# Sample states, pooling and norm sums moved out of the mixer end and under the two input products

## Chip, cores and metric

The kernel runs on one core of a Trainium2 chip. The metric is the device time of one execution in microseconds.

## The reference

One decoder layer for 1024 prompt tokens and 8 sample tokens (1032 together), width 1024, all in float32. The part that the change touches is the mixer:

```python
h = rmsnorm(x, g_mix[l]); proj = h @ w_in[l]
qr, fr, ir, gr, u = jnp.split(proj, ...)           # five blocks of 512 columns
logf = jnp.log(lb + (1.0 - lb) * jax.nn.sigmoid(fr))
kk = (1.0 - lb) * jax.nn.sigmoid(-fr); qq = jax.nn.silu(qr)
o, S = hgrn2_chunked(qq, kk, ir, logf, s_hgrn[l])  # S = diag(f) S + outer(1 - f, i), o = S^T q
o = o * lax.rsqrt(jnp.mean(o * o, axis=-1, keepdims=True) + EPS) * hgrn_norm[l]
y_a = o * jax.nn.sigmoid(gr)
y_b = pool_mix(multiscale_pool(u, past)) * pool_scale[l]   # trailing means over 2, 4, 8, 16 rows
x = x + jnp.concatenate([y_a, y_b], axis=-1) @ w_out[l]
```

Each of the 8 sample tokens has its own old state of 4 heads, 128 x 128, and 15 past rows of u. Cross attention over 256 memory tokens and a SwiGLU block follow.

## The kernel before

The program is written by hand per engine; each engine runs its own list in order, and semaphores join them. TensorE is PE, VectorE is DVE, ScalarE is ACT, GpSimd is POOL, SyncE's queue is SP.

A product is made in stripes of 128 output channels. Each stripe has three thirds of 344 tokens (`chunk`), and each third is 24 matmuls: operands are split into a rounded part and a rest (`w_hi`, `w_lo`, `x_hi`, `x_lo`), and three of the four cross products are summed. For each stripe SP loads the weights into `raw` (two slots), POOL multiplies them by the norm's gains (`gain_stripe`), ACT rounds them into `w_hi` (`split_next`), DVE makes the rest `w_lo` (`split_lo`), and DVE empties each third from its bank (`plain_evac`). A new `raw` may be loaded when the rest of two stripes before is made. ACT rounds a stripe's weights one stripe ahead of its use.

The first stage `qfi` makes q, f and i in 12 stripes. The second, `gu`, makes g and u in 8 stripes, and under each of them lies one step of the recurrence over 128 tokens: TensorE turns the decayed keys and a copy `iv` of v that POOL makes (`turn`, L1664 and L1666), then makes scores and reads the state. For the step of the next stripe ACT makes `lf` and exponentials (`gates`), and DVE runs a scan (`decays`) and four products (`weigh`).

After `gu` comes the mixer end (`mixer_end` on each engine): the new sample states one token at a time, their reads, pooling on POOL (`pooling`, log-step sums in the buffers `pa` and `pb`) with the means on DVE (`means`, L1253), the sums of squares of o (L1746), the norm factors, gating, the pool mix (L1758), and the split of y into `y_hi` and `y_lo`. Only then does the output product start. What POOL's sum for group g may overwrite is guarded by `pooled`, the count of means that DVE has made:

```python
if g and l == (g - 1) % 2:
    pool.wait_ge(pooled, g)
```

Below, "stripe n" of `gu` counts from 0 to 7, and its start is the start of its first third.

## Time and profile before

| | |
|---|---|
| time, three runs | 1551.0 us median (1550.93 to 1552.17) |
| profiled execution | 1551.01 us, span 1549.3 us |
| busy: TensorE, VectorE, ScalarE, GpSimd | 97%, 49%, 21%, 23% of the span |
| mean granted clock of TensorE | 0.99 |
| mixer end | 302.05 to 351.75 us |

A row of the timeline gives start, duration, engine, line, operation, output and inputs with their shapes, a count, and in brackets the idle time before it with what ended it. A matmul on plain float32 shows as two records, a transpose or a matmul on rounded operands as one. Windows give the busy time of PE, PEld (weight loads), DVE, ACT and POOL, each with its count, then the granted clock of TensorE, the share of the DMA engines and GB/s.

### The profile page before, as it was taken

The page shows a single profiled execution, that of the slowest core. Times are in us where ns is not written, and L with a number is a line of the kernel's source. Part 1 is how long each engine was busy: PE and PEld are TensorE (multiplying, and loading weights), DVE is VectorE, ACT ScalarE, POOL GpSimd, SP SyncE. Part 2 cuts the span into 40 slices and gives each one's busy share as a digit, 9 for nine tenths or more (in the row PEclk, how much of TensorE's full clock was granted, in tenths as well). Part 3 has the DMA queues.
Part 4 walks back from the last instruction along what each step waited for, and adds up shares of the span by engine and source line. Part 5 has one row for each costly group of instructions (what it writes and reads, how often), then busy time and mean ns, then how long its engine had stood idle before and what let it go on. Part 6 is the DMA issues. An engine that isn't in the chain of part 4 may idle for free.

```text
span 1549.3 us, 24672 instructions
## 1 busy us (share of the span) xinstructions
PE 1504.4 (97%) x9751; PEld 1465.4 (95%) x9751; DVE 765.6 (49%) x1293; ACT 328.0 (21%) x482; POOL 361.3 (23%) x324
## 2 busy tenths in 40 slices
PE   7999999979999998999999999999999999999998
PEld 6999999949999987779999999999999999999998
DVE  5222666597754276548854454334445422344424
ACT  4023333371020133420121111001111100111111
POOL 2111211154542063005531110001111000111063
PEclk8999999999999998999999999999999999999999
DMA  5111100321151267131111111111111111112113
GB/s 164 42 54 41 42 27 27 81 82 42 41 149 55 68 192 230 64 114 42 54 42 52 43 51 44 41 54 41 45 49 44 51 42 55 41 41 68 34 48 110
DMA packets 155009, 100.98 MB, mean 65 GB/s; under 512 B 9508, under 2 KB 147748, under 8 KB 154947
## 3 DMA queue, kind: packets, MB, share of 16 engines
q1 hardware_dynamic: 154955, 100.24, 21.5%
q8 instruction: 36, 0.59, 0.2%
q14 instruction: 18, 0.15, 0.0%
HBM read 91.50 MB, written 8.96 MB: 65 GB/s over the span
## 4 chain that ended last, share of the span: by engine, by line
PE 84%; DVE 3%; ACT 1%; issue 1%; DMA 0%; DVEq 0%; POOL 0%; SPq 0%; ACTq 0%; POOLq 0%
PE pm L1610 25%; PE pm L1612 24%; PE pm L1611 24%; PE pm L1893 2%; PE pm L1820 2%; PE pm L1918 1%; DVE ssc L1409 1%; PE pm L1679 1%; PE pm L1691 1%; PE pm L1881 1%; PE pm L1717 0%; PE pm L1693 0%; PE pm L1676 0%; DVE vc L1405 0%; PE pm L1983 0%
## 5 line engine op out<-in xcount | busy, mean ns | idle before, releaser
L1610 PE MATMUL pm<-x_hi,w_hi 128*128 128x344 f32 x1728 | 556.1, 322 | 0.2 <-DVE proj L1144 0.2
L1612 PE MATMUL pm<-x_hi,w_lo 128*128 128x344 f32 x1728 | 552.1, 320 | 0.0
L1611 PE MATMUL pm<-x_lo,w_hi 128*128 128x344 f32 x1728 | 552.0, 319 | 0.0
L1610 PEld LDWEIGHTS pm<-x_hi,w_hi 128*128 128x128 f32 x1728 | 324.9, 188 | 1.7 <-issue 0.5
L1611 PEld LDWEIGHTS pm<-x_lo,w_hi 128*128 128x128 f32 x1728 | 324.8, 188 | 0.2
L1612 PEld LDWEIGHTS pm<-x_hi,w_lo 128*128 128x128 f32 x1728 | 325.0, 188 | 0.0
L792 ACT ACTIVATE w_hi<-raw 128x1024 fp32r<-128x1024 f32 x120 | 127.2, 1060 | 855.7 <-PE pm L1612 762.9
L644 POOL TENSOR_TENSOR raw<-raw,gains 128x1024 f32<-128x1024 f32 x72 | 137.9, 1917 | 717.6 <-DMA raw<-in_w_ffn_in 563.6
L1610 PE MATMUL pm<-s_hi,w_hi 128*128 128x344 f32 x528 | 168.9, 320 | 0.0
L1612 PE MATMUL pm<-s_hi,w_lo 128*128 128x344 f32 x528 | 168.7, 319 | 0.0
L1611 PE MATMUL pm<-s_lo,w_hi 128*128 128x344 f32 x528 | 168.5, 319 | 0.0
L1110 DVE TENSOR_TENSOR w_lo<-raw,w_hi 128x1024 fp32r<-128x1024 f32 x112 | 148.8, 1328 | 11.6 <-ACT w_hi L792 11.6
L1610 PEld LDWEIGHTS pm<-s_hi,w_hi 128*128 128x128 f32 x528 | 99.2, 188 | 0.0
L1612 PEld LDWEIGHTS pm<-s_hi,w_lo 128*128 128x128 f32 x528 | 99.2, 188 | 0.0
L1144 DVE TENSOR_TENSOR fa<-pm,rb 128x344 f32<-128x344 f32 x66 | 34.0, 516 | 132.0 <-PE pm L1612 128.6
L1611 PEld LDWEIGHTS pm<-s_lo,w_hi 128*128 128x128 f32 x528 | 99.1, 188 | 0.0
L1144 DVE TENSOR_TENSOR fp<-pm,rb 128x344 f32<-128x344 f32 x66 | 34.1, 516 | 114.6 <-PE pm L1612 114.6
L1144 DVE TENSOR_TENSOR proj<-pm,rb 128x344 f32 (+1 forms) x60 | 30.7, 514 | 114.0 <-PE pm L1612 114.0
L1573 DVE TENSOR_TENSOR acc<-pm,acc 128x344 f32 (+1 forms) x42 | 21.7, 517 | 101.1 <-PE pm L1612 101.1
L1610 PE MATMUL pm<-y_hi,w_hi 128*128 128x344 f32 x192 | 61.5, 320 | 0.7 <-issue 0.7
L1610 PE MATMUL pm<-o_hi,w_hi 128*128 128x344 f32 x192 | 61.6, 321 | 0.0
L1612 PE MATMUL pm<-y_hi,w_lo 128*128 128x344 f32 x192 | 61.3, 319 | 0.0
(261 smaller groups left out, 1969.0 us busy)
## 6 DMA issues: line engine op xcount, KB each, us to landing
raw<-in_w_ffn_in SPq DMA_DIRECT2D x44, 512.0 KB, 3.9
raw<-in_w_in SPq DMA_DIRECT2D x20, 512.0 KB, 3.8
vc<-in_cache_mem_v SPq DMA_DIRECT2D x16, 512.0 KB, 4.3
raw<-in_w_ffn_out SPq DMA_DIRECT2D x16, 512.0 KB, 3.9
xt<-in_x_prompt SPq DMA_DIRECT2D x8, 512.0 KB, 6.0
raw<-in_w_out SPq DMA_DIRECT2D x8, 512.0 KB, 3.9
raw<-in_w_cq SPq DMA_DIRECT2D x8, 512.0 KB, 3.9
vc<-in_cache_mem_k SPq DMA_DIRECT2D x8, 512.0 KB, 5.3
```

Of the source, the lines that this page charges most:

```text
L644: pool.tensor_tensor(raw[:, s, :, :], raw[:, s, :, :], g, ALU.mult).then_inc(gain_on, 1)
L792: act.activation(w_hi[s][:, :, :], src, ACT.Copy).then_inc(hi_made, 1)
L1110: dve.tensor_tensor(w_lo[s][:, :, :], raw[:, s, :, :], w_hi[s][:, :, :].bitcast(F32), ALU.subtract).then_inc(lo_made, 1)
L1144: dve.tensor_tensor(dst, bank[c][:, 0:CH], rb[:, c * CH:(c + 1) * CH], ALU.mult).then_inc(evac, 1)
L1409: dve.tensor_scalar(ssc[:, s, i * H:(i + 1) * H], ssx[:, s, :], 1.0, None, ALU.mult).then_inc(ssc_made, 1)
L1573: dve.tensor_tensor(a, bank[c][:, 0:CH], add, ALU.add).then_inc(evac, 1)
L1610: pe.matmul(out, w_hi[s][:, k, :], hi[:, k, x0:x0 + cols], start=(k == 0), stop=False)
L1611: pe.matmul(out, w_hi[s][:, k, :], lo[:, k, x0:x0 + cols], start=False, stop=False)
L1612: last = pe.matmul(out, w_lo[s][:, k, :], hi[:, k, x0:x0 + cols], start=False, stop=(k == kb - 1))
L1679: last = pe.matmul(bank[6 + x][:, h * P:(h + 1) * P], hg["kt"][x * C:(x + 1) * C, h, :], hg["vt"][x * C:(x + 1) * C, h, :], start=True, st ...
L1820: last = pe.matmul(wide(0)[:, h * XD:(h + 1) * XD], qs[:, 2 * h + d, :], kvT[:, 2 * h + d, :], start=(d == 0), stop=(d == 1))
L1893: last = pe.matmul(wide(4)[:, (2 * h + d) * P:(2 * h + d + 1) * P], vnat[:, a, h * XD + d * P:h * XD + (d + 1) * P], prT[:, 2 * h + a, :], ...
```

## The change

- The stripes of `qfi` come in the order f, i, q, those of `gu` in the order u, g. Both loops are written out instead of looping.
- Sample states: SP loads all eight (and the past rows) behind stripe 5 of `qfi`. POOL scales them in one operation each behind the gains of stripe 7, where ACT used four each. TensorE spreads v by one product per token from a turned and split copy, and DVE adds, under stripes 9 and 10. The reads are 32 products of one column with the state as weights, behind the first third of `gu`. The stores go out under `gu`.
- Pooling of group n-1 stands in POOL's list behind the gains of stripe n+1, its mean in DVE's list behind the weighing at the end of stripe g+2. The past rows' sums are made under stripe 8 of `qfi`, straight from the bank.
- The sums of squares of o are made by thirds of tokens, the first two under stripes 4 and 7 of `gu`, in banks that the recurrence uses, with the factors on ACT and the scaling on DVE; the sigmoid of g comes at the end of `gu`. POOL gates and makes the rests for two thirds of y_a.
- The mixer end keeps mixing by thirds, the last third's sums, factors and gating.
- In the attention, the first stripe of w_co is loaded ahead of the cached values and rounded behind block 1 instead of before the values' natural form.

The diff, cut to its core:

```diff
-MIX_BANKS = (6, 7, 0, 1, 2)
-OSUM_BANKS = (0, 3)
+MIX_BANKS = (4, 5, 6, 7)
+OSUM_BANKS = ((4, 5, 6, 7), (4, 5, 6, 7), (0, 1, 2, 3))
...
+        st = [put(f"st{b}", [P, H, P], at=r0 + 12 * Z + b * 2048) for b in range(NS)]
+        vdup = put("vdup", [P, H, 64], at=r0 + 16 * Z)
+        vn = put("vn", [64, W], F32R, at=r0 + 16 * Z + 1024)
+        past = put("past", [P, W], at=r0 + 16 * Z + 3072)
+        pa = put("pa", [P, TP], at=r0 + 14 * Z)
+        pb = put("pb", [P, TP], at=r0 + 15 * Z)
+        utok = put("utok", [32, W], at=r0 + 13 * Z)
         fs = put("fs", [P, H, NS], at=r1 + 14 * 2048 + 512)
-        otok = put("otok", [H * NS, P], at=r1 + 14 * 2048)
+        psums = put("psums", [P, H, NS], at=r1 + 14 * 2048 + 640)
...
+            if name == "qfi":
+                w, off = t["w_in"], (4 * P if j < 4 else -8 * P)
+            elif name == "gu":
+                w, off = t["w_in"], (16 * P if j < 2 else 8 * P)
...
+                if p is phases[0]:
+                    for i in range(1, p.stripes // 2):
+                        for s in range(2):
+                            load_stripe(p, i, s)
+                        if i == 2:
+                            for b in range(NS):
+                                sp.dma_start(st[b][:, :, :],
+                                             t["state_hgrn"][b].rearrange("h k v -> k h v")).then_inc(old_in[b], 16)
                             sp.dma_start(past[0:NS * PAST, :],
                                          t["state_pool"].rearrange("b r c -> (b r) c")).then_inc(past_in, 16)
+                    continue
...
+                if p.name == "gu":
+                    for n in range(p.stripes):
+                        load_stripe(p, n // 2, n % 2)
+                        if n == 1:
+                            for b in range(NS):
+                                sp.wait_ge(new_made, b + 1)
+                                sp.dma_start(t["hgrn_sample"][b].rearrange("h k v -> k h v"),
+                                             st[b][:, :, :]).then_inc(new_out[b % 4], 16)
+                        if n == 6:
+                            sp.wait_ge(utok_made, 4)
+                            sp.dma_start(t["pool_prompt"][0], utok[0:PAST, :]).then_inc(stored, 16)
+                            sp.dma_start(t["pool_sample"][:, PAST - 1, :], utok[PAST:PAST + NS, :]).then_inc(stored, 16)
+                            sp.dma_start(t["pool_sample"][:, 0:PAST - 1, :], t["state_pool"][:, 1:PAST, :]).then_inc(stored, 16)
+                    sp.wait_ge(b_made, PAIRS)
+                    sp.dma_start(pmix[:, :, :], t["pool_mix"].rearrange("g c d -> c g d")).then_inc(pmix_in, 16)
+                    continue
...
+                    load_stripe(ph["co"], 0, 0)
+                    load_stripe(ph["co"], 0, 1)
                     for s in range(2):
                         load_values(0, s)
-                    load_stripe(ph["co"], 0, 0)
-                    load_stripe(ph["co"], 0, 1)
...
+            def sample_states():
+                pool.wait_ge(fs_made, 1)
+                for b in range(NS):
+                    pool.wait_ge(old_in[b], X_LOADS + (32 if b in (0, 7) else 16))
+                    pool.tensor_tensor(st[b][:, :, :], st[b][:, :, :], fs[:, :, b:b + 1].to_broadcast([P, H, P]),
+                                       ALU.mult).then_inc(old_scaled, 1)
...
+                w = POOLW[g]
+                if g == 0:
+                    for n in range(4):
+                        pool.wait_ge(new_out[n], NEW_STORES)
+                    pool.wait_ge(os_done, 1)
+                pool.wait_ge(evac, ph["gu"].done + NC * (g + 1))
+                cur = u_[:, g, 0:TP]
+                for l in range(g + 1):
+                    dst, sh = (pa, pb)[l % 2][:, :], 1 << l
+                    if g and l == (g - 1) % 2:
+                        pool.wait_ge(pooled, g)
+                    step(pool.tensor_tensor(dst[:, sh:TP], cur[:, sh:TP], cur[:, 0:TP - sh], ALU.add))
+                    step(pool.tensor_copy(dst[:, 0:sh], cur[:, 0:sh]))
+                    cur = dst
+                pool.wait_ge(setup, 11)
+                pool.tensor_tensor(cur[:, 0:w - 1], cur[:, 0:w - 1], early[:, g, 0:w - 1], ALU.mult).then_inc(summed, 1)
+                pool.wait_ge(summed, g + 1)
...
+            def mixer_end():
+                for h in range(H):
+                    pool.wait_ge(o_scaled, 2 * H)
+                    pool.wait_ge(g_act, 1 if h < 3 else 2)
+                    pool.tensor_tensor(q_[:, h, 0:2 * CH], q_[:, h, 0:2 * CH], g_[:, h, 0:2 * CH],
+                                       ALU.mult).then_inc(og_made, 1)
+                for h in range(H):
+                    pool.wait_ge(yhi_made, h + 1)
+                    pool.tensor_tensor(y_lo[:, h, 0:2 * CH], q_[:, h, 0:2 * CH], y_hi[:, h, 0:2 * CH].bitcast(F32),
+                                       ALU.subtract).then_inc(ya_made, 1)
...
+                if p.name == "qfi":
+                    for i in range(p.stripes // 2):
+                        for s in range(2):
+                            gain_stripe(p, i, s)
+                        if i == 3:
+                            sample_states()
+                        if i == 4:
+                            sample_v()
+                elif p.name == "gu":
+                    gain_stripe(p, 0, 0)
+                    for n in range(p.stripes):
+                        v_copy(n // 2, n % 2)
+                        if n + 1 < p.stripes:
+                            gain_stripe(p, (n + 1) // 2, (n + 1) % 2)
+                        if 1 <= n <= H:
+                            pooling(n - 1)
...
+            def squares(c):
+                act.wait_ge(o_out, (4, 7, PAIRS + 1)[c])
+                act.wait_ge(iv_made, (3, 6, PAIRS)[c])
+                if c == 2:
+                    act.wait_ge(os_made, 1)
+                act.activation(i_[:, :, cols(c)], q_[:, :, cols(c)], ACT.Square).then_inc(osq_made, 1)
+            def factors(c):
+                for h in range(H):
+                    act.wait_ge(osum, H * c + h + 1)
+                    act.activation(i_[:, h, cols(c)], bank[OSUM_BANKS[c][h]][:, 0:CH], ACT.Ln, scale=1.0 / P,
+                                   bias=eps[:, 0:1]).then_inc(rn_made, 1)
+                act.wait_ge(rn_made, 5 * c + H)
+                act.activation(i_[:, :, cols(c)], i_[:, :, cols(c)], ACT.Exp, scale=-0.5).then_inc(rn_made, 1)
...
+            for n in range(PAIRS):
+                split_next(p, n // 2, n % 2, n >= 6)
+                if n in (4, 7):
+                    factors(n // 7)
+                kv_read(n // 2, n % 2)
+                if n in (3, 6):
+                    squares(n // 6)
+                if n + 1 < PAIRS:
+                    gates((n + 1) // 2, (n + 1) % 2)
+                if 1 <= n <= H:
+                    u_rows(n - 1)
...
+            for n in range(PAIRS):
...
+                dst = proj[:, 16 + n if n < H else 8 + n, :]
+                if n == H:
+                    for x in range(4):
+                        dve.wait_ge(new_out[x], NEW_STORES)
+                if n == H + 1:
+                    dve.wait_ge(stored, 16 * 3)
+                plain_evac(p, i, s, 0, dst[:, 0:CH])
+                split_lo(nxt(p, i, s, n >= 6))
+                if n == 0:
+                    dve.wait_ge(os_done, 1)
+                    dve.tensor_copy(q_[:, :, TP:T], bank[5][:, 0:H * NS].rearrange("p (h b) -> p h b", h=H)).then_inc(os_made, 1)
+                if n + 1 < PAIRS:
+                    decays((n + 1) // 2, (n + 1) % 2)
+                plain_evac(p, i, s, 1, dst[:, CH:2 * CH])
+                state(i, s, 0)
+                mask(i, s)
+                if n == 7:
+                    scale(1)
+                plain_evac(p, i, s, 2, dst[:, 2 * CH:T])
+                outputs(i, s)
+                state(i, s, 1)
+                if n + 1 < PAIRS:
+                    weigh((n + 1) // 2, (n + 1) % 2)
+                if 2 <= n < 2 + H:
+                    means(n - 2)
+                    sample_mean(n - 2)
+                if n == 5:
+                    scale(0)
...
+                squares(2)
+                round_b(0)
+                for h in range(H):
+                    round_a(h)
...
+                    if i < 7:
+                        split_next(p, i, 1, False)
...
+                        split_next(ph["kv"], 7, 1, True)
...
+            def sample_reads():
+                pe.wait_ge(q_act, H)
+                pe.wait_ge(new_made, NS)
+                for h in range(H):
+                    for b in range(NS):
+                        last = pe.matmul(bank[5][:, h * NS + b:h * NS + b + 1], st[b][:, h, :], q_[:, h, TP + b:TP + b + 1],
+                                         start=True, stop=True)
+                last.then_inc(os_done, 1)
...
+            for n in range(PAIRS):
+                i, s = n // 2, n % 2
+                chunk(ph["gu"], i, s, 0, x_hi, x_lo)
+                if n == 0:
+                    sample_reads()
+                if n in (4, 7):
+                    square_sums(n // 7)
+                    pe.wait_ge(rn_made, 5 * (n // 7) + 1)
+                if n >= 2:
+                    pe.wait_ge(utok_made, min(n - 1, H))
+                turn(i, s)
+                chunk(ph["gu"], i, s, 1, x_hi, x_lo)
+                if n == 0:
+                    pe.wait_ge(os_made, 1)
+                if n in (4, 7):
+                    pe.wait_ge(rn_made, 5 * (n // 7) + H)
+                scores(i, s)
+                if 1 <= n <= H:
+                    turn_u(n - 1)
+                chunk(ph["gu"], i, s, 2, x_hi, x_lo)
+                reads(i, s)
...
+                def mix(c):
+                    for g in range(H):
+                        if c:
+                            pe.wait_ge(yb_made, H * (c - 1) + g + 1)
+                        pe.matmul(bank[MIX_BANKS[g]][:, 0:CH], pmix[:, g, :], u_[:, g, c * CH:(c + 1) * CH],
+                                  start=True, stop=True).then_inc(mixed, 1)
+                pe.wait_ge(pmix_in, 16)
+                pe.wait_ge(pooled, H)
+                pe.wait_ge(spooled, 2 * H + 1)
+                pe.wait_ge(S0_made, PAIRS + 1)
+                mix(0)
...
+                square_sums(2)
+                mix(1)
+                mix(2)
+                pe.wait_ge(rn_made, 15)
+            def y_ready(c):
+                pe.wait_ge(yb_made, H * (c + 1))
+                pe.wait_ge(ya2_made if c == 2 else ya_made, H)
```

GpSimd's list before, where `gu` ends: the last two copies of v in the loop (each turn of the loop is two stripes), and pooling only behind all of them.

```order
L644 TENSOR_TENSOR raw<-raw,gains 128x1024 [waits raw_in1]
L650 REGISTER_ALU [waits evac]
L651 ISA [waits turned]
L651 COPY iv<-proj 128x512
L775 REGISTER_ALU
L775 COMPARE_AND_BRANCH
L671 TENSOR_TENSOR pa<-proj 128x1023 [waits o_done,evac]
L672 COPY pa<-proj 128x1 [waits pool_step]
L676 TENSOR_TENSOR pa<-pa,early 128x1 [waits setup,pool_step]
L671 TENSOR_TENSOR pa<-proj 128x1023 [waits pooled,summed]
```

GpSimd's list now, from the copy for stripe 2 over pooling(1) to the copy for stripe 3 (the second row of `iv`) and the start of pooling(2).

```order
L650 COPY iv<-proj 128x512 [waits turned,evac,summed]
L643 TENSOR_TENSOR raw<-raw,gains 128x1024 [waits raw_in1]
L689 TENSOR_TENSOR pa<-proj 128x1023 [waits pooled,evac]
L690 COPY pa<-proj 128x1 [waits pool_step]
L689 TENSOR_TENSOR pb<-pa 128x1022 [waits pool_step]
L690 COPY pb<-pa 128x2 [waits pool_step]
L694 TENSOR_TENSOR pb<-pb,early 128x3 [waits setup,pool_step]
L650 COPY iv<-proj 128x512 [waits turned,evac,summed]
L643 TENSOR_TENSOR raw<-raw,gains 128x1024 [waits raw_in0]
L689 TENSOR_TENSOR pa<-proj 128x1023 [waits evac]
L690 COPY pa<-proj 128x1 [waits pool_step]
```

Pooling(1) and its wait on `pooled` now stand between two copies of v.

VectorE's list before, from the outputs of a gate stripe over the weighing to the next stripe's second third.

```order
L1207 TENSOR_SCALAR proj<-pm 128x4x128 [waits o_done]
L1200 SCALAR_TENSOR_TENSOR S_91<-S_92,ebs,pm 128x128 [waits S1_made]
L1200 SCALAR_TENSOR_TENSOR S_91<-S_92,ebs,pm 128x128 x3
L1177 TENSOR_TENSOR e_86<-e_86,proj 128x512 [waits exp_e]
L1179 TENSOR_TENSOR e3b<-e3b,proj 128x512 [waits exp_b]
L1181 TENSOR_TENSOR e_82<-e_82,proj 128x512 [waits exp_d]
L1182 TENSOR_TENSOR e_83<-e_83,proj 128x512
L1144 TENSOR_TENSOR proj<-pm,rb 128x344 [waits mm_done]
L1110 TENSOR_TENSOR w_lo_54<-raw,w_hi_52 128x1024 [waits hi_made]
L1144 TENSOR_TENSOR proj<-pm,rb 128x344 [waits mm_done]
```

VectorE's list now, from the outputs of stripe 2 over the weighing for stripe 3 to means(0) (L1304) and the evacuation and `w_lo` under stripe 3.

```order
L1286 TENSOR_SCALAR proj<-pm 128x4x128 [waits o_done]
L1279 SCALAR_TENSOR_TENSOR S_92<-S_93,ebs,pm 128x128 [waits S1_made]
L1279 SCALAR_TENSOR_TENSOR S_92<-S_93,ebs,pm 128x128 x3
L1256 TENSOR_TENSOR e_87<-e_87,proj 128x512 [waits exp_e]
L1258 TENSOR_TENSOR e3b<-e3b,proj 128x512 [waits exp_b]
L1260 TENSOR_TENSOR e_83<-e_83,proj 128x512 [waits exp_d]
L1261 TENSOR_TENSOR e_84<-e_84,proj 128x512
L1304 SCALAR_TENSOR_TENSOR proj<-pa,proj 128x1024 [waits summed,u_turned]
L1311 TENSOR_TENSOR psums<-psums,proj 128x8 [waits spooled]
L1313 SCALAR_TENSOR_TENSOR proj<-psums,proj 128x8 [waits spooled]
L1191 TENSOR_TENSOR proj<-pm,rb 128x344 [waits mm_done]
L1157 TENSOR_TENSOR w_lo_54<-raw,w_hi_52 128x1024 [waits hi_made]
```

The mean that pooling(1) waits for stands behind the outputs of stripe 2 (which need its reads) and behind the weighing; the next evacuation stands behind it.

GpSimd's list now in `qfi`: the last three of the eight scalings of states, then the gains of stripes 8 and 9 and the start of the copy of v.

```order
L657 TENSOR_TENSOR st_100<-st_100,fs 128x512 [waits load_in5]
L657 TENSOR_TENSOR st_101<-st_101,fs 128x512 [waits load_in6]
L657 TENSOR_TENSOR st_102<-st_102,fs 128x512 [waits load_in0]
L643 TENSOR_TENSOR raw<-raw,gains 128x1024 [waits raw_in0]
L643 TENSOR_TENSOR raw<-raw,gains 128x1024 [waits raw_in1]
L662 MEMSET vdup 128x256
```

Before, the gains of these stripes followed those of stripes 6 and 7 with nothing between.

## Rows read from the trace of the kernel before

**Rows 1.** Page, part 1: busy us (share of the span), instructions per engine.

```profile
PE 1504.4 (97%) x9751; PEld 1465.4 (95%) x9751; DVE 765.6 (49%) x1293; ACT 328.0 (21%) x482; POOL 361.3 (23%) x324
```

**Rows 2.** Whom TensorE waited for: us in total, times, longest.

```profile
PE pm L1881 <- ACT vnat L1029: 4.3, 1, 4.3
...
PE pm L1664 <- DVE e L1177: 2.8, 1, 2.8
```

**Rows 3.** Window from the last gate stripe's end to the output product.

```profile
302.05:351.75 49.70, 35.43 (x188) 24.43 (x188) 44.19 (x80) 36.16 (x58) 26.61 (x24) 0.97 0.27 75
```

**Rows 4.** Timeline of TensorE inside it: start, us, instruction.

```profile
304.14 2.05 PE L1717 MATMUL pm<-ident,proj 128*128 128x128 f32 x16 [0.34 <-DVE S L1200]
...
336.64 2.00 PE L1746 MATMUL pm<-proj,ones 128*128 128x344 f32 x6 [1.06 <-ACT proj L900]
```

**Rows 5.** Timeline of TensorE in a gate stripe.

```profile
285.10 0.41 PE L1610 MATMUL pm<-x_hi,w_hi 128*128 128x344 f32 x1
...
288.95 0.60 PE L1664 MATMUL pm<-ident,e 128*128 128x128 f32 x4
...
295.67 0.42 PE L1610 MATMUL pm<-x_hi,w_hi 128*128 128x344 f32 x1
```

**Rows 6.** Timeline of VectorE: scan and mask of one stripe, last weighing, a mean.

```profile
259.02 1.45 DVE L1163 TENSOR_TENSOR_SCAN b<-keep,lf 128x512 f32<-128x512 f32 x1 [1.96 <-ACT lf L848]
...
263.17 0.73 DVE L1186 COPY_PREDICATED am<-cmask,pm 128x512 f32<-128x512 int32 x1
...
288.78 0.68 DVE L1182 TENSOR_TENSOR e<-e,proj 128x512 f32<-128x512 f32 x1
...
305.29 1.22 DVE L1253 SCALAR_TENSOR_TENSOR proj<-pa,proj 128x1024 f32<-128x1024 f32 x1
```

**Rows 7.** Timeline of ScalarE in the gate stripe that starts at 251.15.

```profile
255.96 0.60 ACT L871 ACTIVATE kt<-pm 128x512 f32<-128x512 f32 x1 [6.26 <-PE pm L1666]
...
258.36 0.63 ACT L848 ACTIVATE lf<-proj 128x512 f32 x1
```

**Rows 8.** Timeline of GpSimd: pooling of group 1, first and last.

```profile
306.65 1.89 POOL L671 TENSOR_TENSOR pa<-proj 128x1023 f32<-128x1023 f32 x1 [1.75 <-DVE proj L1253]
...
311.10 0.20 POOL L676 TENSOR_TENSOR pb<-pb,early 128x3 f32<-128x3 f32 x1
```

**Rows 9.** GpSimd's groups by shape: busy us, mean ns.

```profile
L644 POOL TENSOR_TENSOR raw<-raw,gains 128x1024 f32<-128x1024 f32 x72 | 137.9, 1917 | 717.6 <-DMA raw<-in_w_ffn_in 563.6 <-DMA raw<-in_w_in 110.1 <-DMA raw<-in_w_cq 43.1
...
L729 POOL TENSOR_TENSOR keep<-keep 128x64 f32<-128x64 f32 x8 | 2.6, 320 | 69.9 <-PE pm L1918 44.5 <-DVE keep L1468 25.4
```

**Rows 10.** One line, GpSimd's copies of i: ns min/median/max.

```profile
L651 POOL COPY iv<-proj x8: 611/1324/1433, 162.5 to 273.1; 128x512 f32 x8
```

**Rows 11.** Windows after the first turn: busy us; the clock behind POOL.

```profile
168.00:170.00 2.00, 1.80 (x9) 1.80 (x10) 1.65 (x4) 2.00 (x4) 0.00 (x0) 0.50 0.00 0
170.00:172.00 2.00, 2.00 (x10) 2.00 (x10) 2.00 (x3) 1.81 (x4) 1.43 (x2) 0.67 0.02 4
```

**Rows 12.** Timeline of TensorE: products of one moving column.

```profile
1528.90 0.66 PE L1994 MATMUL pm<-ones,sqfin 128*128 128x1 f32 x6
```

**Rows 13.** Timeline of TensorE: two spreads of 512 columns.

```profile
597.11 0.73 PE L1837 MATMUL pm<-qn,sel 64*128 64x512 f32 x2
```

**Rows 14.** Timeline of ScalarE in the first product stage, one stripe.

```profile
116.42 1.06 ACT L792 ACTIVATE w_hi<-raw 128x1024 fp32r<-128x1024 f32 x1 [10.27 <-PE pm L1612]
```

**Rows 15.** Timeline of SyncE's queue: five loads of states.

```profile
276.23 4.71 SPq L491 DMA_DIRECT2D proj<-in_state_hgrn  x5
```

**Rows 16.** ScalarE's groups by shape.

```profile
L1074 ACT ACTIVATE fa<-fa 128x344 f32<-128x344 f32 x66 | 32.0, 487 | 137.1 <-DVE fa L1144 137.1
...
L912 ACT ACTIVATE proj<-proj 128x4128 f32<-128x4128 f32 x1 | 3.6, 3644 | 0.0
```

**Rows 17.** Timeline of ScalarE at the start of the attention.

```profile
608.26 1.06 ACT L792 ACTIVATE w_hi<-raw 128x1024 fp32r<-128x1024 f32 x1 [8.45 <-DMA raw<-in_w_co]
```

**Rows 18.** Window there.

```profile
608.00:618.50 10.50, 7.01 (x32) 6.64 (x33) 2.77 (x11) 6.68 (x13) 2.92 (x10) 0.51 0.71 236
```

More of the change, by code:

```diff
@@ L131, in hybrid_layer @@
         comb = put("comb", [P, 32])
+        sel = put("sel", [64, NS], F32R)
         rtok = put("rtok", [P, 16])
@@ L1329, in mixer_end @@
                 rest_b(1)
-                rest_a(3)
+                for h in range(H):
+                    rest_a2(h)
                 rest_b(2)
-                rest_b(3)
             def residual(p):
```

501 lines of the change are left out of this document (184 added, 317 removed).

## The prediction

> **What bounds the kernel now.** The page first: TensorE is busy 97% of the span, VectorE 49%, ScalarE 21%, GpSimd 23% [rows 1]. So a step counts by what it does to TensorE's time. The waits of TensorE name two that matter here: 2.8 us on VectorE's `e` at the first turn of the gate product, and 4.3 us on ScalarE's `vnat` as the attention starts [rows 2]. The windows then show the mixer end: from the last gate stripe (302.05) to the output product (351.75) are 49.70 us, with VectorE busy for 44.2, ScalarE for 36.2 and TensorE for 35.4 on small products [rows 3]. The rest of TensorE's time is products that the change leaves alone. I time the gate stripes, where much of the work goes, from their start (0). A stripe takes 16.95 us (285.10 to 302.05) [rows 3, 5]: columns 0 to 343; the turn at 3.85; thirds and scores until the last third starts at 10.57; 3.85 later, at 14.4, the reads; all done at 16.95 [rows 5]. In the stripe that starts at 251.15, VectorE's mask ends at 12.75, 1.65 before the reads need it [rows 6]. ScalarE goes from the first read of the turned keys to the end of `lf` in 3.03 us (255.96 to 258.99), and VectorE from its scan to the third's evacuation, state and mask in 4.9 [rows 6, 7]. VectorE's last weighing for the next stripe starts 3.68 after that stripe's start and is over at 4.36 [rows 5, 6].
>
> **1. First product stage, +9.** TensorE gets four turns of v (8 records; 16 took 2.05 us, so 1.0 [rows 4]), four turns of the past rows (half as many records, 0.5) and eight spreads of 512 columns (two took 0.73 less the last one's tail, 0.33 each, 2.6 [rows 13]): 4.1. Then a wait. GpSimd scales the eight states before it may do stripe 8's gains, and it waits with them for `fs`, which comes after the last evacuation of stripe 6, 1.1 us into stripe 7. One scaling of 512 columns lies between the 64 columns of 0.32 us and the 1023 of 1.89 us [rows 8, 9]: 1.06, and with 0.07 between two, 9.0 for eight. The gains take 1.92 [rows 9], ScalarE's rounding 1.06 [rows 14], VectorE's rest 1.2. I take 0.1 for each hand-over. 1.2 + 9.0 + 2.0 + 1.2 + 1.3 makes stripe 8's weights ready at 14.7, and a stripe is 11.33 long (10.27 + 1.06 [rows 14]): 3.4 us of wait. The bounds are 0 (the scalings cost half) and 5. SyncE's queue takes nine loads here, behind those of stripe 5: five took 4.71 us [rows 15], so nine 8.5, inside the 11.33 before the next weights' slot is free.
>
> After a wait the clock is low. Behind the first turn's 2.8 us the granted clock was 0.50 for 2 us and 0.67 for the next 2 [rows 11], that is 1.2 instead of 2.4 GHz for some 3.3 us, so 1.6 us lost. In the attention it stayed at 0.51 over 10.5 us, with 7.0 busy: 3.5 us lost [rows 18]. I take 1.6 for each long wait that full product work follows, and 3.5 as the upper bound. Sum of the stage: 4.1 + 3.4 + 1.6 = 9.1.
>
> **2. First gate stripe, +2.6.** `sample_reads` is 32 products of one column, each two records. Six such records take 0.66 us, 0.11 each [rows 12]: 64 make 7.0. They stand where TensorE waited 2.8 [rows 2] and lost 1.6 by the clock. ScalarE's last silu comes later than the work there now, but `e` is made about 7.4 us into the stripe (silu 1.1, table and `lf` 1.9, scan to `d` 2.7, exponential and weighing 1.3, evacuation 0.5), and the reads end at 10.9. So 7.0 − 4.4 = +2.6. Here the Trainium skill differs, on its page "TensorE: Matmul & The Clock Gate": Part 2 puts a product's throughput at its moving columns alone, and Part 1 gives about 25 ns as the floor between two. By it the 64 records would take 1.6 us. The rows say 0.11, with 128 weight columns loaded each time, and the measurement decides.
>
> **3. Small work under the gates, +5.3.** The sums of squares of two thirds: six records took 2.00 [rows 4], so eight take 2.4, twice 4.8. Four turns of u are 0.5. The eight state stores stand on SyncE's queue ahead of the third gate stripe's weights; at the loads' 0.94 each they are 7.5 us, and three times that would still be early. GpSimd's pooling(0) and VectorE's stripe 4 wait for them, more than 17 us later. VectorE's stripe 5 waits for the pool stores, which follow ScalarE's last rows of u; that is close, but lies under the longer wait of part 4.
>
> **4. The pooling chain, +33.** This is the largest term. In GpSimd's order, pooling(1) stands before the copy of v for stripe 3, and begins with a wait for means(0). VectorE does means(0) at the end of its stripe 2, behind the reads and behind the weighing: it starts 4.3 into stripe 3 and takes 1.22 [rows 6], so GpSimd is let go at 5.65. Pooling(1) takes 4.65 (306.65 to 311.30 [rows 8]), the copy 0.61 at best and 1.43 at worst [rows 10]: `iv` is there at 11.1, and the turn, ready at 3.85, waits 7.3. The clock adds 1.6. Behind the copy stand the gains of stripe 4 (1.9), behind those ScalarE's rounding, squares(0) (1376 columns at 3.64 us for 4128 [rows 16], 1.35) and `lf`; the mask comes at 23.7 and costs 0.2. With 0.1 for a turn of u already counted, stripe 3 loses 9.1.
>
> Stripe 4: pooling(2) must wait for means(1) ahead of its second level; its two last levels take as long as pooling(1), so `iv` comes at 11.1 again. But the turn also needs bank 4, freed by the first logarithm of factors(0), and ScalarE stands before it with the rounding of stripe 5, for which GpSimd's gains come at 13.0. 13.0 + 0.1 + 1.06 + 0.5 + 0.1 = 14.8, against 6.2 (3.85 and the sums): 8.6, and 1.6: 10.2. Stripe 5: pooling(3) waits for means(2) at once and has four levels, twice 4.65 less one early product, 9.15: `iv` at 15.6, so 11.8 and 1.6: 13.4. Stripes 6 and 7 have no pooling; scale(0) and squares(1) use up the mask's 1.65 there and no more. Sum 32.7; with 0.4 for smaller hand-overs I take 33. A copy at 1.43 adds 2.4. On contention the Trainium skill, page "SBUF — State Buffer", section "Who interferes with whom", has GpSimd and VectorE exclude each other on one port pair; the copy's spread from 0.61 to 1.43 [rows 10] agrees. That speaks against pooling under the gates, but my chain runs while VectorE itself waits, so it is in the upper bound only.
>
> **5. Mixer end, −30.7.** What is left, from the end of the last reads (0): outputs and state give TensorE its start at 2.1 (304.14 less 302.05 [rows 3, 4]); mix(0) 2.4, square_sums(2) 2.4, mix(1) 2.4, to 9.3. ScalarE rounds the first mix until 5.1, rounds y's first two thirds (four of 688 columns, 0.7) to 7.9, four logarithms of 344 columns (0.45 of 0.49 [rows 16]) to 9.7, one exponential of 1376 to 11.1. VectorE: scale(2), gate2 and rest_b(1), four each at 0.46, to 16.7. Then mix(2)'s last product, 17.4, and TensorE's idle 6 us cost 1.6 by the clock: 19.0 against 49.7. GpSimd's last rest of y (11.7) is covered. ScalarE and VectorE set this, so without their cover nothing more is lost; the bounds are 16 and 24.
>
> **6. Attention start, −7.5.** ScalarE's rounding of w_co waited 8.45 us for its load [rows 17] with `vnat` queued behind it, and TensorE stood still for 4.3 [rows 2]. The rounding is moved behind block 1 and the load ahead of the values. TensorE then waits 0.2 and not 4.3, and the low clock's 3.5 go with it. Bounds 4.3 and 7.8.
>
> **The sum.** 9.1 + 2.6 + 5.3 + 33 − 30.7 − 7.5 = +11.8. The profiled execution took 1551.0 (span 1549.3), which is the median too: **1562.8 us**.
>
> **The rivals.**
> *The chain is hidden* (faster). If GpSimd came to its copies in time, the 33 fall away: 1530. For it: GpSimd is busy for 23% only, and pooling needs 24 us of four stripes. Against it: the order of the two engines, in which each copy stands behind a wait for a mean of the stripe that just ended. It decides at 21 us of lost time in stripes 3 to 5 together, a third less than my sum. 10%, with all else that ends below 1547.9.
> *Gains and losses meet*, within 0.2% (3 us, about what a measurement of this kernel can tell from no change): 4%.
> *The low clock lasts* as in the attention: five waits at 3.5 and not 1.6 give +9.5, 1572. For it, rows 18; against it, there TensorE had more gaps, and behind mine stand 4 us of product without one. 14%.
> *One-column products are cheap*: if a record costs next to nothing beside its one column, the reads are over soon after 3.85, the turn waits for `e` until 7.5 and stripe 0 comes 3.4 earlier: 1559.4. Against it are rows 12; 4%. It is what the page of the Trainium skill named in part 2 would make of it.
> *The forecast*: 68%.
>
> **How the numbers follow.** The forecast's own range is 1555 to 1571 (first stage −5, mixer end −3 to +5, copies +2.4, attention +3). To hold eight in ten I reach to the low clock's case above and leave out the hidden chain below: 1553 to 1574. Slower is the forecast, the lasting clock and the cheap products: 0.86; same 0.04; faster 0.10.
>
> **What would show it.** Right: turns of stripes 3, 4 and 5 waiting 7, 9 and 12 us, with GpSimd idle until a mean and then pooling; stripe 8 waiting for `w_lo` some 3 us; no wait at the first turn; a mixer end near 19; no wait on `vnat`. Wrong: gate stripes of 17 us throughout, or a mixer end over 25.

## The result, and the profile after

The changed kernel takes 1573.1 us (1572.84 to 1573.50) against 1551.6 in the same session: a ratio of 1.0139, 95% interval 1.0122 to 1.0157, 21.5 us slower. The forecast was 1562.8, slower, in a range of 1553 to 1574. So the direction and the range held and the size was little more than half. The time is near that of the rival in which the low clock lasts (1572), but not by its mechanism alone. One execution among the experiments below, in the first run of all repairs together, had a mean granted clock of 0.75 and took 1839.9 us; it is left out of that run's figures.

The page of the changed kernel, part 1, and whom TensorE waited for (us in total, times, longest), which answer to [rows 1, 2]:

```profile
PE 1509.3 (96%) x9702; PEld 1471.5 (94%) x9702; DVE 755.0 (48%) x1299; ACT 321.0 (20%) x467; POOL 375.1 (24%) x344
...
PE pm L1746 <- POOL iv L650: 19.3, 2, 12.1
PE pm L1746 <- ACT proj L943: 8.1, 1, 8.1
PE pm L1832 <- DVE y_lo L1368: 7.2, 1, 7.2
...
PE pm L1656 <- DVE w_lo L1157: 2.3, 1, 2.3
...
PE pm L1960 <- ACT vnat L1075: 0.3, 1, 0.3
```

The waits are the three of the forecast's chain (7.2, 8.1 and 12.1), one in the mixer end and one in the first stage; of those in [rows 2] the one on `e` is gone and the one on `vnat` is down from 4.3 to 0.3. Windows of the gate product, one for each stripe, and of the mixer end (last row):

```profile
169.29:199.91 30.62, 30.62 (x195) 30.38 (x193) 13.57 (x23) 12.70 (x19) 6.65 (x5) 0.78 0.06 18
199.91:216.98 17.07, 17.07 (x131) 16.81 (x131) 10.94 (x21) 6.52 (x11) 3.75 (x5) 1.00 0.11 32
216.98:234.07 17.09, 17.09 (x132) 16.83 (x131) 10.83 (x21) 5.46 (x10) 0.00 (x0) 1.00 0.11 32
234.07:260.96 26.89, 19.70 (x131) 19.21 (x131) 12.83 (x24) 7.64 (x12) 9.72 (x9) 0.81 0.07 20
260.96:291.36 30.40, 22.29 (x139) 20.90 (x139) 12.47 (x24) 9.61 (x16) 6.82 (x7) 0.83 0.08 23
291.36:322.78 31.42, 19.33 (x130) 18.84 (x130) 14.01 (x24) 7.41 (x11) 13.88 (x13) 0.78 0.01 4
322.78:339.83 17.05, 17.05 (x131) 16.79 (x130) 14.50 (x28) 7.18 (x11) 0.96 (x1) 1.00 0.28 78
339.83:359.15 19.32, 19.32 (x138) 18.23 (x137) 10.40 (x22) 11.43 (x13) 2.52 (x2) 1.00 0.01 2
359.15:380.32 21.17, 12.04 (x36) 7.45 (x35) 13.71 (x28) 14.47 (x26) 10.36 (x7) 0.84 0.14 38
```

Stripes 3, 4 and 5 have the waits. Stripe 0 is the one to look at: 30.62 us long, TensorE busy for all of it, and the granted clock at 0.78. Its middle, by windows and by the timeline:

```profile
173.10:175.10 2.00, 2.00 (x21) 2.00 (x19) 1.84 (x3) 0.02 (x1) 0.00 (x0) 1.00 0.00 0
175.10:184.60 9.50, 9.50 (x48) 9.50 (x48) 4.81 (x8) 3.24 (x6) 0.00 (x0) 0.52 0.18 55
184.60:191.40 6.80, 6.80 (x34) 6.80 (x35) 1.94 (x3) 3.00 (x4) 2.47 (x2) 0.67 0.00 0
```
```profile
173.13 11.57 PE L1784 MATMUL pm<-proj,st 128*128 128x1 f32 x64
184.57 1.09 PE L1746 MATMUL pm<-ident,e 128*128 128x128 f32 x4
```

The 64 records of `sample_reads` take 11.57 us. For the first 2 the clock is at 1.00; then it falls to 0.50, 1.2 instead of 2.4 GHz, although TensorE waits for nothing, and the turn and part of the next third run at it too.

Where the 22.1 us between the two profiled executions (spans 1549.3 and 1571.4) went, with the forecast beside it:

| part | forecast | measured | how |
|---|---|---|---|
| 1 first product stage | +9.1 | +7.9 | third 2 of its last stripe evacuated at 169.55, was 161.68 |
| 2 gate stripe 0 | +2.6 | +9.1 | the next starts at 199.91, was 182.90 |
| 3, 4 gate stripes 1 to 7 | +38.3 | +40.1 | 159.2, was 119.15 |
| 5 mixer end | −30.7 | −28.5 | 21.2, was 49.7 |
| 6 attention, and the rest | −7.5 | −6.5 | remainder |
| sum | +11.8 | +22.1 | |

### The profile page after: what moved, and what is told of

Read it like the earlier page. It is cut to its first block, busy times and chain, and to the rows that moved or that the text cites. A ratio compares the mean times of both kernels' runs of the same rounds, so it can differ in the third digit from the quotient of the medians.

```text
span 1571.4 us, 24244 instructions
## 1 busy us (share of the span) xinstructions
PE 1509.3 (96%) x9702; PEld 1471.5 (94%) x9702; DVE 755.0 (48%) x1299; ACT 321.0 (20%) x467; POOL 375.1 (24%) x344
## 4 chain that ended last, share of the span: by engine, by line
PE 93%; DVE 3%; POOL 2%; ACT 1%; issue 1%; SPq 0%; DMA 0%; DVEq 0%; POOLq 0%; ACTq 0%
PE pm L1656 27%; PE pm L1658 27%; PE pm L1657 27%; PE pm L1972 2%; PE pm L1899 2%; PE pm L1997 1%; PE pm L1784 1%; PE pm L1761 1%; PE pm L1773 1%; POOL st L657 1%; POOL pb L689 1%; POOL pa L689 0%; PE pm L1960 0%; PE pm L1832 0%; PE pm L1775 0%
## 5 line engine op out<-in xcount | busy, mean ns | idle before, releaser
L1157 DVE TENSOR_TENSOR w_lo<-raw,w_hi 128x1024 fp32r<-128x1024 f32 x112 | 152.6, 1362 | 48.2 <-ACT w_hi L837 48.2
L1191 DVE TENSOR_TENSOR proj<-pm,rb 128x344 f32<-128x344 f32 x60 | 30.6, 514 | 101.6 <-PE pm L1658 101.5
L1657 PE MATMUL pm<-o_lo,w_hi 128*128 128x344 f32 x192 | 61.3, 319 | 0.0
```

Source lines behind the costliest of these rows:

```text
L1157: dve.tensor_tensor(w_lo[s][:, :, :], raw[:, s, :, :], w_hi[s][:, :, :].bitcast(F32), ALU.subtract).then_inc(lo_made, 1)
L1191: dve.tensor_tensor(dst, bank[c][:, 0:CH], rb[:, c * CH:(c + 1) * CH], ALU.mult).then_inc(evac, 1)
L1657: pe.matmul(out, w_hi[s][:, k, :], lo[:, k, x0:x0 + cols], start=False, stop=False)
```

## The experiments

"The ratio" is always against the kernel before on the same chip; that of the change is 1.0139.

**One part undone at a time.** The means of the pooled groups, earlier in VectorE's list:

```diff
                 split_lo(nxt(p, i, s, n >= 6))
+                if 2 <= n < 2 + H:
+                    means(n - 2)
...
                 if 2 <= n < 2 + H:
-                    means(n - 2)
                     sample_mean(n - 2)
```

> The mean of group n-2 is taken right behind the weights' rest at the start of gate stripe n instead of at its end; nothing else changes. Theory (GpSimd's copies of v stand behind a wait for a mean of the stripe that just ended): the three waits of the turns of stripes 3, 4 and 5 (7.2, 8.1 and 12.1 us) and the low clock behind each go, stripes 3 and 5 take about 17.1 us and stripe 4 about 19.6 (with the sums of squares), and the time is 1573.1 - 35 = 1538 us. Rival (it is the 24 us of pooling as such, beside VectorE's work, that the stripes pay for): stripes 3 to 5 stay above 19 us each without a turn's wait on iv, and the time is above 1548.

Measured: 1542.4 us (1538.23 to 1543.27), ratio 0.9927 (0.9910 to 0.9945). The three waits are gone, stripe 5 is at 17.06, and 31 of the 35 us came, by the medians (the four executions spread over 5 us). Its stripes 2 to 5, a new entry in the list of TensorE's waits, and VectorE in stripe 2:

```profile
217.21:235.25 18.04, 17.36 (x132) 16.81 (x131) 14.48 (x22) 6.63 (x11) 10.44 (x9) 1.00 0.11 30
235.25:253.58 18.33, 17.37 (x131) 16.83 (x131) 13.76 (x24) 7.87 (x12) 8.62 (x8) 1.00 0.10 30
253.58:274.25 20.67, 19.70 (x140) 18.33 (x139) 14.17 (x24) 8.99 (x15) 12.43 (x11) 1.00 0.05 15
274.25:291.31 17.06, 17.06 (x130) 16.80 (x130) 13.97 (x24) 7.42 (x11) 5.16 (x3) 1.00 0.10 30
```
```profile
PE pm L1774 <- DVE am L1265: 2.6, 3, 1.0
```
```profile
225.19 2.18 DVE L1242 TENSOR_TENSOR_SCAN b<-keep,lf 128x512 f32<-128x512 f32 x1 [0.94 <-ACT lf L896]
227.41 0.69 DVE L1246 TENSOR_TENSOR lf<-b 128x512 f32<-128x512 f32 x1
228.01 2.38 DVE L1248 TENSOR_TENSOR d<-b 128x512 f32<-128x512 f32 x1
...
230.74 1.11 DVE L1279 SCALAR_TENSOR_TENSOR S<-S,ebs,pm 128x128 f32<-128x128 f32 x4
231.78 0.72 DVE L1265 COPY_PREDICATED am<-cmask,pm 128x512 f32<-128x512 int32 x1
```

Pooling was running on GpSimd from 224.40 to 230.71. The scan took 2.18 instead of 1.23 and `d` 2.38 instead of 0.69; together 2.65, less the slack of 1.65 that the mask has [rows 5, 6]: 1.0, and the stripe is 18.04 instead of 17.07. So both theories hold a part: nearly all was the wait, and some 1 us for each of stripes 2 to 4 is the collision (0.95, 1.24 and 1.1 over what was expected, 3.3 together). The mean itself lies in VectorE's idle time before the scan and costs nothing. The rest of what is missing from the 35 lies elsewhere. In the mixer end the first mix waits 1.9 us in both kernels; in the changed kernel (first row) it then ran at the full clock, here (second row) it did not, 1.6 us more:

```profile
361.31 2.55 PE L1832 MATMUL pm<-proj,keep 128*128 128x344 f32 x8 [1.91 <-DVE S L1279]
```
```profile
329.82 4.12 PE L1833 MATMUL pm<-proj,keep 128*128 128x344 f32 x8 [1.90 <-DVE S L1279]
```

Only stripe 8's gains ahead of the scalings of states (`sample_states()` called behind the gains of `(4, 0)`, not behind those of stripe 7):

> GpSimd makes the gains of stripe 8 of the first product stage ahead of the eight scalings of states instead of behind them. Theory (the wait of 2.34 us for the weights' rest at stripe 8 is the scalings' queue, and it cost no clock, since the granted clock stayed at 1.00 behind it): that wait goes and the time falls by 2.3 us to 1570.8. Rival (the wait is for the weights' load, which stands on SyncE's queue behind nine loads of states): no change within 0.5 us.

Measured: 1570.1 (1567.92 to 1571.17), ratio 1.0110 (1.0093 to 1.0127). The intervals of the two ratios overlap, so the size is not shown by the times; the list of TensorE's waits no longer has the 2.3 on `w_lo`, and the span is 1569.4. The loads were not what was late.

The attention's part alone, on the kernel before:

```diff
+                    load_stripe(ph["co"], 0, 0)
+                    load_stripe(ph["co"], 0, 1)
                     for s in range(2):
                         load_values(0, s)
-                    load_stripe(ph["co"], 0, 0)
-                    load_stripe(ph["co"], 0, 1)
...
-                    split_next(p, i, 1, i == p.stripes // 2 - 1)
+                    if i < 7:
+                        split_next(p, i, 1, False)
...
+                        split_next(ph["kv"], 7, 1, True)
```

> The kernel before with the attention's part of the change alone: w_co's first stripes loaded ahead of the cached values, and the rounding moved behind block 1. Theory: TensorE's wait of 4.3 us for vnat goes, and with it the low clock over the first block; in the changed kernel this part gave 6.5 us, so the time is 1551.5 - 6.5 = 1545. Rival (only the wait goes and the clock stays low for the other gaps there): 1547.2.

Measured: 1545.9 (1544.49 to 1546.59), ratio 0.9956 (0.9940 to 0.9973): 7.0 us, and no wait on `vnat`. This part is a gain on its own.

**What the reads cost.** Two runs of 32 records instead of one of 64 (`sample_reads((0, 1))` behind the first third, `sample_reads((2, 3))` behind the second, with the copy of their sums behind that third's evacuation):

> The reads of heads 0 and 1 stay behind the first third of gate stripe 0, those of heads 2 and 3 move behind its second third, and VectorE's copy of their sums moves behind the second third's evacuation. Theory (a record of a one-column product takes 0.095 us at the full clock; it is the granted clock that falls to 0.50 after some 2 us of an unbroken run of them, and stays there for 64 records and the product behind): two runs of 32 records take about 3.1 to 4 us each, stripe 0 falls from 30.6 us to about 24, and the time is about 1566.5. Rival (a record costs 0.18 us in itself): the two runs take 5.8 us each and the time stays within 1 us of 1573.

Measured: 1571.1 (1570.28 to 1572.71), ratio 1.0122 (1.0105 to 1.0139). The interval overlaps that of the change, so the times show no gain; in the profile stripe 0 took 27.8 us, not the 24 expected. The rows:

```profile
173.86 3.64 PE L1784 MATMUL pm<-proj,st 128*128 128x1 f32 x32
177.41 1.12 PE L1746 MATMUL pm<-ident,e 128*128 128x128 f32 x4
...
183.66 3.63 PE L1784 MATMUL pm<-proj,st 128*128 128x1 f32 x32
187.58 2.08 PE L1758 MATMUL pm<-e,e 128*128 128x128 f32 x8 [0.28 <-DVE proj L1338]
```
```profile
173.90:177.40 3.50, 3.50 (x33) 3.50 (x31) 3.25 (x5) 1.47 (x4) 0.00 (x0) 0.99 0.00 0
177.40:183.70 6.30, 6.30 (x35) 6.30 (x35) 4.72 (x6) 4.78 (x7) 3.45 (x2) 0.73 0.18 54
183.70:187.30 3.60, 3.59 (x33) 3.51 (x31) 2.06 (x4) 1.26 (x3) 0.00 (x0) 1.00 0.17 51
187.30:191.30 4.00, 3.72 (x24) 3.41 (x24) 0.19 (x1) 0.00 (x0) 0.00 (x0) 0.57 0.02 4
```

A record is 0.114 at the full clock, not 0.18: the rival's price is wrong. But my 6.5 us were wrong too: stripe 0 gave 2.8, and 1.5 of them went again behind the wait before the first mix (4.00 for its 2.55). Each run of 3.6 us still brought the clock down, now behind itself, where the turn takes 1.12 instead of 0.60 and the scores 2.08 instead of 1.05. Shorter runs, one head each, three of them in the last stripe of the first stage:

```diff
+                    if m == 11:
+                        sample_reads(c)
...
-                    sample_reads()
+                    sample_reads(H - 1)
```

> The reads of one head each (16 records) stand behind the three thirds of the last stripe of the first product stage and behind the first third of gate stripe 0. Theory (a record costs 0.11 us at the full clock; two runs of 3.64 us each still brought the clock down behind them, runs of 1.8 us between thirds of 4 us may not): three runs of 1.8 us at a granted clock of 1.00; in stripe 0 1.8 us of reads and then a wait for e until 7.3 us into the stripe with 1.6 us of low clock behind it. All reads and waits then cost 7.0 + 1.6 + 1.6 = 10.2 us where they cost 13.7, and the time is about 1569.6. Rival (the clock falls behind every such run too): the low clock costs about 1.6 us behind each of four runs, and the time is 1574 or more.

Measured: 1567.3 (1566.72 to 1568.20), ratio 1.0098 (1.0081 to 1.0115), 5.8 us under the change where 3.5 were expected. The wait for `e` that the theory had did not come: the third run lies between the last third and the stripe, so the chain to `e` had 1.8 us more, and the turn starts at 180.73 without a wait. All windows from the first run to the scores have a granted clock of 1.00; the first and the last run:

```profile
162.20:164.00 1.80, 1.80 (x19) 1.80 (x17) 1.56 (x2) 0.00 (x0) 0.00 (x0) 1.00 0.00 0
...
179.00:180.70 1.70, 1.70 (x17) 1.70 (x16) 1.54 (x4) 1.45 (x4) 0.00 (x0) 1.00 0.00 0
180.70:182.00 1.30, 1.30 (x13) 1.30 (x13) 0.99 (x2) 1.30 (x3) 0.04 (x1) 1.00 0.00 0
```

And the reads at their place, but with 128 moving columns each:

```diff
-                        last = pe.matmul(bank[5][:, h * NS + b:h * NS + b + 1], st[b][:, h, :], q_[:, h, TP + b:TP + b + 1],
+                        last = pe.matmul(bank[5][:, h * P:(h + 1) * P], st[b][:, h, :], q_[:, h, b * P:(b + 1) * P],
```

> The 32 reads of states at their place, but each with 128 moving columns of prompt q instead of one column of a sample's q (the sample tokens' o is then not the layer's; everything else is). Theory (the clock falls because almost no columns are moved, not for the place or the weight loads): 64 records of about 0.13 us, 8.4 us, at a granted clock of 1.00, no low clock behind; 128 times the columns take less time than one column, stripe 0 falls from 30.6 to about 25.4 us and the time to 1568. Rival (any long run on loaded states brings the clock down, or products are simply priced by columns): 64 records take over 11.6 us and the time is 1573 or more.

Measured: 1566.5 (1565.72 to 1568.05), ratio 1.0091 (1.0074 to 1.0107).

```profile
174.97 7.31 PE L1784 MATMUL pm<-proj,st 128*128 128x128 f32 x64
182.11 0.60 PE L1746 MATMUL pm<-ident,e 128*128 128x128 f32 x4
```

128 times the columns take 7.31 us instead of 11.57, 0.114 a record, with the clock at 1.00 throughout. Stripe 0 took 24.6 us where 25.4 were expected. So a one-column record costs what one of 128 columns costs as long as the clock holds, and it is the run of one-column products, not the place or the number of records alone, that brought the clock down. The page "TensorE: Matmul & The Clock Gate" of the Trainium skill, Part 2, puts throughput at one moving column a cycle; the trace does not agree for these shapes, where the column count changed nothing. The same part of the page prices the load of the weights by itself, at 107 ns for 128 columns (an estimate by its formula), and 0.114 a record lies near that. That it is the load which sets the price is not shown: no run here varied it.

**The mixer end.** The third mix behind the output product's first third, and VectorE's `rest_b(1)` ahead of its last scaling:

```diff
                 mix(1)
-                mix(2)
...
             def y_ready(c):
+                if c == 1:
+                    mix(2)
...
                 rest_b(0)
+                rest_b(1)
                 scale(2)
                 for h in range(H):
                     gate2(h)
-                rest_b(1)
```

> The changed kernel with the third mix moved behind the first third of the output product, and VectorE's second rest of y's pooled half ahead of the last scaling. Theory (the wait of 7.2 us before the third mix is only the order: what the product's first third needs is there 0.1 us after GpSimd's last rest of y, 12.5 us into the mixer end): the output product starts at 12.6 us instead of 21.2, gives 2.4 us back for the third mix, and the time falls by about 6 us to 1567. Rival (the chain over VectorE to the last rest only moves behind the second third): TensorE waits 5 us or more before the last third of the first stripe or for the second stripe's weights, and the time falls by under 2 us.

Measured: 1567.9 (1566.68 to 1568.02), ratio 1.0099 (1.0082 to 1.0116): 5.2 us. The wait of 7.2 became one of 3.4, and the third ran in 3.8 us at the full clock.

**Where GpSimd and VectorE collide.** Two more runs on the means. Behind the mask for groups 0, 1 and 3:

> The early mean of the first experiment, but for groups 0, 1 and 3 it stands behind the mask of the stripe instead of behind the weights' rest; group 2 stays there. In the first experiment gate stripes 2 to 5 took some 1.1 to 1.3 us more than 17.07 each, TensorE waiting for the mask. Theory (the mean's 1.2 us in front of the scan pushes the mask past the reads): stripes 2, 3 and 5 go back to about 17.1 us, and the time falls from 1542.4 to about 1539. Rival (it is pooling on GpSimd beside VectorE that makes VectorE late): the stripes keep their 18 us and the time stays at 1542.

Measured: 1543.4 (1542.28 to 1546.15), ratio 0.9949 (0.9933 to 0.9966), no gain over 0.9927. Stripes 2, 3 and 5 did go to 17.1, but the mean of group 1 now lets pooling(2) go so late that the gains of stripe 5 are late, and stripe 4 waits 2.4 us for the first logarithm of `factors(0)`. The theory was right for the stripes and wrong for the sum: the wait moved.

> The early means of the first experiment, with GpSimd's sums of groups 2 and 3 made for 8 columns only instead of some 1020 (what is left out: the pooled halves of those groups are wrong); group 1's are whole, as a control. Theory (GpSimd's sums and VectorE's operations on two tensors in memory hold each other up: VectorE's d took 2.38 us beside pooling and 0.69 without, and the mask comes late by that): d is 0.69 in gate stripes 3 and 4 and stays 2.38 in stripe 2, stripes 3 and 4 lose 1.2 us each, stripe 2 stays at 18.0, and the time is 2.4 us under the first experiment's, about 1540. Rival (the mean's own 1.2 us ahead of the scan makes the mask late): stripes 3 and 4 stay 1 us or more over 17.07 and the time within 0.8 us of the first experiment's.

Measured: 1541.7 (1540.77 to 1542.76), ratio 0.9936 (0.9919 to 0.9952): by the times not told from the first experiment. Stripe 4 fell by 0.9 to 19.76 (252.45 to 272.21), with `d` at 0.68 but the scan at 2.32. Stripe 3 took 18.20, was 18.33: with the sums gone, the gains on GpSimd fell on VectorE's `lf` instead:

```profile
244.79 2.20 DVE L1247 TENSOR_TENSOR lf<-b 128x512 f32<-128x512 f32 x1
```
```profile
243.64 2.81 POOL L643 TENSOR_TENSOR raw<-raw,gains 128x1024 f32<-128x1024 f32 x1
```

This one is a miss in both theories: the gains, a large operation of GpSimd too, do it as well as the sums.

**All repairs together**, first with group 0's mean behind the mask:

> All repairs together: the reads by head between thirds, stripe 8's gains ahead of the scalings, the third mix behind the output product's first third, the means early (group 0 behind the mask of stripe 2, groups 1 to 3 behind the weights' rest of stripes 3 to 5). If the parts add, from the ratios against the kernel before: early means -31, reads -6, gains -2.3 to -3, mix -5.5, and 1 for stripe 2: 1573 - 46 = 1527 us, 1.6% below the kernel before. Rival (they overlap: one wait hides another): over 1532.

Measured: 1532.4 (1531.95 to 1535.11, three executions), ratio 0.9881 (0.9862 to 0.9901). The sum of the parts was 5.4 us too good, and the rival's 1532 is just reached. Stripe 3 took 21.9 us: it had pooling beside the weighing, a wait of 2.3 us for the mask and the low clock behind it. Then as in the first experiment, and with the means behind the scan:

> The combination of all repairs, but with the mean of group 0 behind the weights' rest too, as in the first experiment. In the combination before, pooling of group 1 began late and ran beside VectorE's weighing (two of its operations took 2.38 us instead of 0.68), and stripe 3 took some 22.4 us with a wait of 2.3 us for the mask and the low clock behind it. Theory (collisions of GpSimd's and VectorE's operations count only where VectorE has no slack): stripes 2 and 3 take 18.0 and 18.3 us again, and the time falls from 1533.8 to about 1530.5. Rival (the 3 us over the sum of the parts lie elsewhere): it stays within 1 us of 1533.8.

> The same combination with the means of groups 0, 1 and 3 right behind the scan and its two differences, so that GpSimd's sums run beside the state update and the mask, which read from the banks and took no longer beside pooling (1.11 and 0.71 us). Theory: lf and d take 0.69 each, the mean's 1.2 us uses up the mask's slack of 1.65, stripe 2 takes 17.1 us and not 18.0, stripe 3 about 18, stripe 4 stays near 20.7, and the time is 1 to 1.5 us under the one beside it, about 1529. Rival (the mean in front of the state update costs what the collision did): no difference over 0.5 us.

Measured: 1529.8 (1529.10 to 1532.01) and 1530.4 (1529.64 to 1530.95), both with ratio 0.9865 (0.9848 to 0.9881, and 0.9849 to 0.9882): 1.35% faster than the kernel before. The two intervals overlap each other and that of the run before, so the ranking of the three combinations is not shown by the times. In the first, stripes 2 and 3 took 18.04 and 18.34 us, as expected. The second did what was expected in the stripes (2 to 4 take 56.0 us instead of 57.05, `d` and `lf` 0.69 in stripes 2 and 3) and lost it later, so its expected gain of 1 to 1.5 us is a miss. The wait before the output product and the third behind it, in the first and in the second:

```profile
330.40:333.70 3.30, 0.00 (x0) 0.00 (x0) 1.08 (x3) 3.27 (x6) 3.15 (x2) 1.00 0.00 0
333.70:337.80 4.10, 4.04 (x25) 4.07 (x26) 4.10 (x10) 0.95 (x3) 0.00 (x0) 1.00 0.02 4
```
```profile
328.60:331.80 3.20, 0.02 (x1) 0.00 (x0) 1.08 (x3) 3.17 (x6) 3.04 (x2) 0.85 0.00 0
331.80:338.50 6.70, 6.65 (x25) 6.68 (x26) 6.31 (x14) 1.97 (x5) 0.00 (x0) 0.56 0.01 2
```

The same wait, 3.4 and 3.2 us, costs no clock in one and 2.6 us (6.7 against 4.1) in the other.

## Why the forecast was half right

**Part 1** (+9.1, measured +7.9). The queue of eight scalings was read rightly from the lists: they took 8.11 us (9.0 in the forecast), the wait 2.34 (3.4). No low clock followed it (1.6 in the forecast). What I left out is that five of the six interruptions of the stage cost some 0.2 us beside their own records: with two spreads (0.65) behind it, a third takes 4.62 us instead of 3.77, and the turns of v add 1.24 for 1.0. Only the turns of the past rows (0.43 for 0.5) do not. Together that is 1.0 of the 1.5 us that the small work came out over the forecast's 6.4 (4.1 and a wait of 2.34).

**Part 2** (+2.6, measured +9.1) **is the step that failed**, with 6.5 of the 10.3 us. The price of a record, 0.11, was right (0.114). Wrong was to count all 64 at the full clock and to put the low clock behind them at nothing, because TensorE would no longer wait. It did not wait, and the clock fell all the same: the records took 11.57 and not 7.0, and the turn and the third behind them 2.1 more. 11.57 + 2.1 − 4.4 = 9.3. The experiments with two runs, four runs and wide reads show the cause. The rival of cheap one-column products had it the wrong way round.

**Part 3** held: the sums of squares cost stripe 7 2.3 us (2.4 forecast), and stripes 1, 2 and 6 are at 17.05 to 17.09. The stores of states delayed nobody.

**Part 4** (+33) was right in mechanism and size. Turns waited 7.19, 8.12 and 12.09 us where the forecast has 7.3, 8.6 and 11.8; the second on the logarithm, as forecast. Low clock behind each cost 2.6, 2.8 and 2.3 us (26.89 − 17.09 − 7.19 and so on, in stripe 4 less the sums' 2.3) and not 1.6. Against 17.02 us a stripe before, part 4 measured some 35.3 and part 3 some 4.8 (5.3 in the forecast), together the +1.8. The first experiment undid the waits. The collisions, which I left out because VectorE waits too, stayed off TensorE's path here: all eight `d` of the changed kernel take 0.68 to 0.69, and though the weights' rest takes 1.75 instead of 1.21 beside pooling in stripe 3 (at 248.04), nothing waited for it. They come onto the path when the wait is repaired, and cost 3.3 us; with the 1.6 at the first mix they are why the repair gives 30 us between the two profiled executions and not 35.

**Part 5** (−30.7, measured −28.5), 2.2 us mis-sized. VectorE could start its last scaling at 11.1 us, as forecast, but its four operations took 3.19 and not 1.84: GpSimd was making its rests of y (365.19 to 371.63). So the collisions that I had put at nothing were on the path in this place. And I added 1.6 us of low clock to the last product only, where all four of the third mix lay behind the wait:

```profile
370.27 3.19 DVE L1320 SCALAR_TENSOR_TENSOR proj<-proj,hnorm 128x344 f32<-128x344 f32 x4 [5.22 <-ACT proj L946]
```
```profile
375.71 4.79 PE L1832 MATMUL pm<-proj,keep 128*128 128x344 f32 x8 [7.22 <-DVE y_lo L1368]
```

**Part 6** (−7.5, measured −7.0 alone; the −6.5 of the change is only what the other parts leave) held.

**The rivals.** The lasting clock had the better time, partly for a wrong reason: it lasted longer behind the long waits (2.3 to 2.8 us) but its largest cost came where nothing waited. That the range held was luck in part: its upper end stood for 3.5 us of low clock behind five waits, and 6.5 of the 10.3 us that filled it came from part 2, where no wait was. The parts named for the narrower range add up to +10.4 and so to 1573, not to the 1571 given. The hidden chain is refuted. That experiments which mend the order reach 1529.8, near that rival's 1530, is a different thing: the change's work does fit under the gates, its order did not.

## What to carry to other kernels

Moving work under a product is free only if each engine's list lets it: follow, for each operation that is moved, what stands behind it and whether it waits for something that the same stripe makes last. Here one line in VectorE's list was worth 31 us. Price a run of thin products at the low clock as well, and put it between full ones in short pieces. After mending a wait, look for what the wait had kept apart.

## What the runs showed of the hardware

- The granted clock fell to 0.50 about 2 us into a run of one-column products with TensorE busy throughout; a run of 128-column products of the same number and place kept it at 1.00. Runs of 16 records (1.84 us) between full thirds kept it too. Runs of 32 (3.64 us) kept it to their end, and it fell behind them (0.53 from 177.4 to 181.0 behind the first, 0.57 behind the second).
- A wait of 2 to 3.4 us may or may not be followed by the low clock: none behind 2.34, 3.37 and 3.40 us, about 2.6 us lost behind one of 3.23. The plainest case is the wait of 1.9 us before the first mix, which the changed kernel and all eleven experiments on it have: in five of the twelve profiles the eight records behind it took 2.55 us, in seven 3.65 to 4.24. A timing model to 1 us is not to be had from such waits. What decides it stays open.
- A VectorE operation with both operands in memory took longer beside a large GpSimd operation (`d` 2.38 for 0.69, the scan 2.18 for 1.23), and GpSimd's took longer as well (gains 2.81 for 1.9). In stripe 2 of the first experiment `d` ended 0.55 us after the sum beside it did, as if it had stood still until then. The state update and the mask, which read a bank, kept their 1.11 and 0.72. This agrees with the Trainium skill, page "SBUF — State Buffer", section "Who interferes with whom": an instruction of VectorE with two inputs in that memory contends with GpSimd's reads, one with at most one such input, outside its two-port modes, does not.
